# Token slots per work item in an expert loop: 128 becomes 96

## The chip, the core and the metric

The kernel runs on one core of a Trainium2 chip. The metric is the device time of one launch in microseconds (us). Of the kernel before there are three timed runs: 2023.76, 2024.81 and 2032.89 us, median 2024.81 us. The profile is one further execution, taken by the hardware profiler.

## What is computed

The reference is a chain of three transformer-like blocks on 256 tokens (plus 16 meta tokens in the first block) of width 1024, all in float32. The change touches one stage of the first block, the mixture of experts behind the pooling layer:

```python
def moe_swiglu(h, w_router, e_gate, e_up, e_down):
    logits = (h @ w_router).astype(jnp.float32)
    top_vals, top_idx = lax.top_k(logits, TOP_K)          # TOP_K = 2
    top_w = jax.nn.softmax(top_vals, axis=-1)
    combine = ...                                          # token x expert weights
    for e in range(N_EXPERTS):                             # N_EXPERTS = 8
        y = y + combine[..., e:e + 1] * swiglu(h, e_gate[e], e_up[e], e_down[e])
```

`swiglu` is `(silu(h @ w_gate) * (h @ w_up)) @ w_down` with a hidden width of 3584. Only the last 256 of the 272 tokens are needed from here on. Each of them goes to two experts, so there are 512 (token, expert) pairs for eight experts, 64 per expert on the average. The reference's router, evaluated on the inputs that the reference draws with seed 0, sends 47, 72, 65, 72, 61, 58, 74 and 63 tokens to the eight experts. With the seeds 1 to 5 the fullest expert gets 79, 92, 86, 76 and 93.

## The kernel before

**Precision.** Nearly all large products are split into three fast products. A float32 operand is taken apart into a high part, rounded to the fast float32 format (fp32r), and a low part, which is what the rounding lost. A product is then high x high + high x low + low x high, three matmuls that add into one PSUM bank.

**Weights.** A stream of chunks of 1 MB (128 partitions x 2048 float32) is fetched by the DMA queue of SyncE into a ring of six slots (`ring`). For each chunk ScalarE writes the high part (`split_moe`, L1592) into one of six other buffers (in the tiles `high` and `scr_r`), and VectorE writes the low part over the slot in the ring (`split_low`, L1935). TensorE then uses both. SyncE may refill a slot as soon as TensorE has begun on the chunk after it (semaphore `moe_begun`).

**Items.** The tokens are sorted by expert into 512 slots ahead of the loop (`sort_tokens`, L870). The loop works on items. An item is one expert and up to `CAP` of its slots. An expert with more than `CAP` tokens gets two items or more and its weights are fetched again for each; an expert with fewer still gets one. VectorE works out the number of items from the counts (`make_places`, `make_table`, L2047 to L2071), and every engine loops over that number, read from a register.

**Inside an item** there are 42 chunks in 14 units of 256 hidden columns (`UNITS`). In `gate_up` (L920, L923, L924) the stationary operand is the item's tokens, 128 input features x `CAP` tokens (`x_item_high`, `x_item_low`), and the moving operand is 512 columns of weights, so the result has `CAP` rows. ScalarE takes the silu of the gate half (L1611), VectorE multiplies by the up half (L2135). `turn_hidden` (L931) transposes the result by two TensorE transposes into PSUM, 128 hidden x `CAP` tokens each. ScalarE and VectorE take their high and low parts from there (L1598, L2123). In `down` (L945, L948, L949) these are the stationary operand, and the weights with 512 columns are the moving one. Once per item TensorE also makes the matrix that puts the rows back to their tokens (L962), and adds the previous item's outputs into `x` (`sum_outputs`, L894, L895, and L2106 on VectorE).

**Between items** ScalarE scales the finished rows (L1580) and VectorE takes their low part (L2112), and the next item's tokens are picked from the slots at a start read from a register (L1613, L2138, L2139). ScalarE also loads its function table for silu at the head of each item (L1584). Ahead of the first item the picks are made from PSUM (L1564 to L1569, L2084).

The order of the instructions on each engine is written out by hand. `MOE_ORDER` is the order of the chunks, and the splits run `LOOK` = 3 chunks ahead of TensorE. `ps[0:CAP, ...]`, `hid[0:CAP, ...]` and the like show that the rows of the hidden and of the output tiles are the item's slots.

Of the kernel before, what the change touches and what calls it, by code (L numbers as in the profile page):

```python
# [23 lines left out]
E_FF = 3584  # L24
KE = E_FF // P
NE = 8
CAP = 128
MAX_ITEMS = NE + 2 * SEQ // CAP
SLOTS = 2 * SEQ
WIDE = 256  # L30
# [169 lines left out]
def program(nc, w_stream, vec_in, h_in, out):  # L200
    with ExitStack() as ctx:
# [65 lines left out]
        x_tok_low = sq_old_r[:, 0:2 * D].rearrange("p (t d) -> p t d", t=2)  # L267
        slots_high = big[:, 0:KD * SLOTS + CAP]
        slots_low = big[:, 4224:4224 + KD * SLOTS + CAP]
        x_item_high = big_r[:, 8448:8448 + KD * CAP].rearrange("p (k c) -> p k c", k=KD)  # L270
        x_item_low = big_r[:, 9472:9472 + KD * CAP].rearrange("p (k c) -> p k c", k=KD)
        hn_old_r = hn_r[:, :, :].rearrange("p k t -> p (k t)")
        picks = hn_old_r[:, 1024:1024 + 2 * SLOTS + CAP]
        pick = picks[:, 0:2 * SLOTS].rearrange("p (t c) -> p t c", t=2)
# [2437 lines left out]
```

## Time and profile before

| | |
|---|---|
| median of three runs | 2024.81 us |
| span of the profiled execution | 2023.5 us |
| TensorE busy | 1981.8 us (98%), 12238 matmuls |
| VectorE busy | 1496.9 us (74%) |
| ScalarE busy | 1187.3 us (59%) |
| moved by DMA | 510.23 MB, mean 252 GB/s |
| experts' loop | about 378 to 1344 us of the span |

The spans are in microseconds from the first instruction. "PE" is the matmul side of TensorE and "PEld" its weight load, meaning the load of the stationary operand, which overlaps the matmul before it. A form such as `128*128 128x512` is the stationary operand (partitions * columns) and the moving one (partitions x columns). DVE is VectorE, ACT is ScalarE, POOL is GpSimd. A row of the windows view gives the stretch and its length, then the busy time of PE, PEld, DVE, ACT and POOL with the number of instructions, the granted clock as a share of full speed, the DMA share and GB/s; for one line alone only the engines that it runs on. The end of a matmul is modelled, its start is recorded, so the pace of TensorE is read from starts.

### The profile page before, as it was taken

The numbers are of one execution on the slowest core, as the hardware profiler recorded it, in microseconds if no ns is written. First come the engines' busy times: TensorE is split into PE (matmuls) and PEld (weight loads), VectorE is DVE, ScalarE is ACT, GpSimd is POOL, SyncE is SP. The second block draws the span as 40 slices with busy tenths as digits, with TensorE's granted clock in tenths as the row PEclk, the third lists the DMA queues.
The fourth block names the chain that finished last, engine by engine and source line by source line (L and its number), as shares of the span: only waits on it lengthen the run. The fifth ranks groups of instructions, "written<-read, shape, count | busy, mean of one in ns | idle before, by whom it ended". The sixth has DMA issues, their size and how long they took to land.

```text
span 2023.5 us, 31645 instructions
## 1 busy us (share of the span) xinstructions
PE 1981.8 (98%) x12238; PEld 1736.5 (86%) x12238; DVE 1496.9 (74%) x1628; ACT 1187.3 (59%) x1269; POOL 58.3 (3%) x105
## 2 busy tenths in 40 slices
PE   8999999999999999999999999999999999999997
PEld 7699998788888888888888888889978879989997
DVE  7776554888999999899899999977484358446652
ACT  5164443778777787777778777773363355325442
POOL 3020000000000000000000000010000000030000
PEclk9999999999999999999999999999999999999999
DMA  6535453499999999999999999974523324445551
GB/s 253 170 126 179 176 194 119 159 365 373 352 373 363 365 371 361 370 365 365 364 364 376 357 372 363 364 269 169 185 100 110 125 105 146 167 147 187 188 183 47
DMA packets 75863, 510.23 MB, mean 252 GB/s; under 512 B 8320, under 2 KB 14464, under 8 KB 14592
## 3 DMA queue, kind: packets, MB, share of 16 engines
q1 hardware_dynamic: 75776, 508.98, 67.7%
q8 instruction: 66, 1.08, 0.2%
q14 instruction: 21, 0.17, 0.0%
HBM read 506.66 MB, written 2.29 MB: 252 GB/s over the span
## 4 chain that ended last, share of the span: by engine, by line
PE 83%; DVE 5%; ACT 4%; issue 3%; DMA 3%; SPq 1%; POOL 0%; ACTq 0%; DVEq 0%; POOLq 0%
PE ps L920 9%; PE ps L924 9%; PE ps L923 9%; PE ps L652 8%; PE ps L655 8%; PE ps L656 8%; PE ps L945 4%; PE ps L949 4%; PE ps L948 4%; PE ps L629 3%; PE ps L1211 2%; PE ps L1214 2%; PE ps L1213 2%; DMA spread<-big 2%; PE ps L1146 1%
## 5 line engine op out<-in xcount | busy, mean ns | idle before, releaser
L1935 DVE TENSOR_TENSOR ring_r<-ring,high 128x2048 fp32r<-128x2048 f32 x227 | 517.8, 2290 | 53.6 <-ACT high L1592 32.7
L1592 ACT ACTIVATE high<-ring 128x2048 fp32r<-128x2048 f32 x224 | 428.6, 1913 | 15.1 <-DMA ring<-w_stream 14.7
L1808 DVE TENSOR_TENSOR ring_r<-ring,high 128x2048 fp32r<-128x2048 f32 x115 | 263.3, 2293 | 123.5 <-ACT high L1395 123.3
L923 PE MATMUL ps<-ring_r,big_r 128*128 128x512 f32 x896 | 349.1, 390 | 0.0
L655 PE MATMUL ps<-scr_r,high 128*128 128x256 f32 (+1 forms) x1200 | 342.6, 285 | 0.0
L1395 ACT ACTIVATE high<-ring 128x2048 fp32r<-128x2048 f32 x115 | 218.7, 1908 | 163.7 <-PE ps L652 92.3
L1935 DVE TENSOR_TENSOR ring_r<-ring,scr_r 128x2048 fp32r<-128x2048 f32 x112 | 256.4, 2290 | 39.0 <-ACT scr_r L1592 38.7
L652 PE MATMUL ps<-sq_r,high 128*128 128x272 f32 (+1 forms) x832 | 238.2, 286 | 5.5 <-DVE scr_r L1826 5.5
L656 PE MATMUL ps<-sq_r,ring_r 128*128 128x272 f32 (+1 forms) x832 | 237.7, 286 | 0.0
L655 PEld LDWEIGHTS ps<-scr_r,high 128*128 128x128 f32 x1200 | 227.1, 189 | 0.2
L1592 ACT ACTIVATE scr_r<-ring 128x2048 fp32r<-128x2048 f32 x112 | 214.5, 1915 | 17.8 <-DMA ring<-w_stream 17.8
L920 PE MATMUL ps<-high,big_r 128*128 128x512 f32 x512 | 205.2, 401 | 0.9 <-ACT big_r L1569 0.9
L924 PE MATMUL ps<-high,big_r 128*128 128x512 f32 x512 | 200.2, 391 | 0.0
L923 PEld LDWEIGHTS ps<-ring_r,big_r 128*128 128x128 f32 x896 | 168.8, 188 | 31.5
L652 PEld LDWEIGHTS ps<-sq_r,high 128*128 128x128 f32 x832 | 157.4, 189 | 6.7 <-issue 4.7
L656 PEld LDWEIGHTS ps<-sq_r,ring_r 128*128 128x128 f32 x832 | 157.0, 189 | 0.0
L920 PE MATMUL ps<-scr_r,big_r 128*128 128x512 f32 x384 | 154.1, 401 | 0.0
L924 PE MATMUL ps<-scr_r,big_r 128*128 128x512 f32 x384 | 150.1, 391 | 0.0
L924 PEld LDWEIGHTS ps<-high,big_r 128*128 128x128 f32 x512 | 96.1, 188 | 21.2
L920 PEld LDWEIGHTS ps<-high,big_r 128*128 128x128 f32 x512 | 96.2, 188 | 19.3 <-issue 1.4
L652 PE MATMUL ps<-hn_r,high 128*128 128x256 f32 (+1 forms) x368 | 109.3, 297 | 0.7 <-DVE scr_r L1832 0.5
L656 PE MATMUL ps<-hn_r,ring_r 128*128 128x256 f32 (+1 forms) x368 | 103.8, 282 | 0.0
(484 smaller groups left out, 3797.1 us busy)
## 6 DMA issues: line engine op xcount, KB each, us to landing
ring<-w_stream SPq DMA_DIRECT2D x477, 1024.0 KB, 4.8
big<-spread SPq DMA_DIRECT2D x32, 146.0 KB, 3.1
spread<-big SPq DMA_DIRECT2D x8, 151.0 KB, 5.4
h<-h_in SPq DMA_DIRECT2D x1, 1088.0 KB, 5.1
out<-hn SPq DMA_DIRECT2D x1, 1024.0 KB, 4.7
vec<-vec_in SPq DMA_DIRECT2D x1, 576.0 KB, 8.1
```

The costliest lines, as they stand in the source:

```text
L652: mm = pe.matmul(o, w_high[:, cols], x_high[:, k, 0:t], start=(k == 0), stop=False)
L655: pe.matmul(o, w_high[:, cols], x_low[:, k, 0:t], start=False, stop=False)
L656: mm = pe.matmul(o, w_low[:, cols], x_high[:, k, 0:t], start=False, stop=(k == kt - 1))
L920: mm = pe.matmul(o, x_item_high[:, k, :], w_high[:, cols], start=(k == 0), stop=False)
L923: pe.matmul(o, x_item_high[:, k, :], w_low[:, cols], start=False, stop=False)
L924: mm = pe.matmul(o, x_item_low[:, k, :], w_high[:, cols], start=False, stop=(k == KD - 1))
L945: mm = pe.matmul(o, hid_t_high[u % 3][:, kk, :], w_high[:, cols], start=first, stop=False)
L948: pe.matmul(o, hid_t_high[u % 3][:, kk, :], w_low[:, cols], start=False, stop=False)
L1395: act.activation(parts_at(c, 0, CH)[0], blocks_at(c, 0, CH), ACT.Copy).then_inc(S["weights_high"], 1)
L1592: act.activation(w_high, w, ACT.Copy).then_inc(S["moe_high"], 1)
L1808: dve.tensor_tensor(w_low, blocks_at(c, 0, CH), w_high.bitcast(F32), ALU.subtract).then_inc(S["weights_low"], 1)
L1935: dve.tensor_tensor(w_low, w, w_high.bitcast(F32), ALU.subtract).then_inc(S["moe_low"], 1)
```

## The change

One constant: `CAP`, the number of token slots of an item, goes from 128 to 96. Everything else follows from it.

```diff
@@ -24,7 +24,7 @@
 E_FF = 3584
 KE = E_FF // P
 NE = 8
-CAP = 128
+CAP = 96
 MAX_ITEMS = NE + 2 * SEQ // CAP
 SLOTS = 2 * SEQ
 WIDE = 256
```

What follows from it:

- The stationary operands of `gate_up`, `down` and L962 have 96 columns instead of 128. Their moving operands keep 512 (144 in L962) columns.
- `turn_hidden` transposes 96 rows instead of 128. The stationary operand is then 96 partitions * 128 columns, the moving one 96 x 96 (a corner of the identity) instead of 128 x 128.
- `sum_outputs` multiplies over 96 partitions instead of 128.
- ScalarE and VectorE handle 192 elements per partition instead of 256 in L1598 and L2123, and 768 instead of 1024 in L1613 and L2138. In L1611, L2135, L1580 and L2112 the elements per partition stay, on 96 partitions instead of 128.
- `make_places` compares the counts with 96 and also with 192 (the loop of L2048 now runs once; before it was empty): one more VectorE instruction on 128 x 8.
- `MAX_ITEMS` goes from 12 to 13. An expert with more than 96 tokens now takes a second item.

## Rows read from the trace of the kernel before

**Rows 1.** The page: busy time and granted clock in tenths, 40 slices.
```profile
PE 1981.8 (98%) x12238; PEld 1736.5 (86%) x12238; DVE 1496.9 (74%) x1628; ACT 1187.3 (59%) x1269; POOL 58.3 (3%) x105
...
PEclk9999999999999999999999999999999999999999
```

**Rows 2.** Windows: engines' busy time (instructions), clock, DMA share, GB/s; two items, ten us.
```profile
741.90:862.30 120.40, 120.32 (x551) 99.10 (x550) 109.49 (x82) 91.33 (x75) 0.00 (x0) 1.00 0.96 366
862.30:982.80 120.50, 120.40 (x551) 99.11 (x550) 109.62 (x82) 91.32 (x75) 0.00 (x0) 1.00 0.96 365
...
700.00:710.00 10.00, 10.00 (x46) 8.25 (x45) 9.64 (x9) 7.89 (x7) 0.00 (x0) 1.00 1.01 389
```

**Rows 3.** Chain of waits inside an item: start us, us, what.
```profile
691.07 0.23 PE ps L923
...
696.74 0.23 PE ps L924
696.97 0.22 PE ps L931 x2
```

**Rows 4.** Windows over the whole loop, for L920 alone and for L948 alone.
```profile
378.00:1345.00 967.00, 359.26 (x896) 168.34 (x896) 1.00 0.96 364
...
378.00:1345.00 967.00, 174.28 (x448) 84.14 (x448) 1.00 0.96 364
```

**Rows 5.** Groups by line and form, weight loads: count, busy us, mean ns.
```profile
L923 PEld LDWEIGHTS ps<-ring_r,big_r 128*128 128x128 f32 x896 | 168.8, 188 | 31.5
...
L722 PEld LDWEIGHTS ps<-big 128*32 128x32 f32 x384 | 13.0, 115 | 14.1 <-DMA big<-spread 4.9 <-issue 1.3
...
L1135 PEld LDWEIGHTS ps<-h,big 128*64 128x64 f32 x144 | 7.6, 136 | 2.3 <-issue 2.0
```

**Rows 6.** Chain of waits in stages with 128 x 256 moving operands.
```profile
1389.95 0.12 PE ps L652
...
1396.00 0.12 PE ps L652
...
1579.87 2.16 PE ps L629 x10
```

**Rows 7.** Timeline of weight loads around a pair of transposes: start us, us.
```profile
696.58 0.37 PEld L931 LDWEIGHTS ps<-ident,h 128*128 128x128 f32 x2
696.92 0.19 PEld L920 LDWEIGHTS ps<-high,big_r 128*128 128x128 f32 x1
697.03 0.19 PEld L923 LDWEIGHTS ps<-ring_r,big_r 128*128 128x128 f32 x1
```

**Rows 8.** Groups by line and form, matmul side of the small products.
```profile
L931 PE MATMUL ps<-ident,h 128*128 128x128 f32 x224 | 43.1, 274 | 2.4 <-DVE h L2135 2.1
...
L962 PE MATMUL ps<-h_r 128*128 128x144 f32 x16 | 3.4, 294 | 0.0
```

**Rows 9.** Timeline of TensorE at the first transposes of an item.
```profile
755.54 0.39 PE L924 MATMUL ps<-scr_r,big_r 128*128 128x512 f32 x1
756.01 0.44 PE L931 MATMUL ps<-ident,h 128*128 128x128 f32 x2
```

**Rows 10.** Chain of waits that leads to those transposes.
```profile
733.98 1.06 ACT big_r L1613
...
736.73 0.37 ACT h_r L1598
...
753.00 0.42 DVE big_r L2123
```

**Rows 11.** Groups of one item, 741.9 to 862.3 us, ScalarE and VectorE.
```profile
L1592 ACT ACTIVATE high<-ring 128x2048 fp32r<-128x2048 f32 x28 | 53.6, 1914 | 1.7 <-DMA ring<-w_stream 1.6
...
L1613 ACT ACTIVATE big_r<-big 128x1024 fp32r x1 | 1.1, 1055 | 0.0
...
L2106 DVE TENSOR_TENSOR x<-ps,x 128x512 f32<-128x512 f32 x4 | 2.7, 683 | 0.0
...
L2123 DVE TENSOR_TENSOR big_r<-ps,big_r 128x256 fp32r<-128x256 f32 x5 | 2.1, 418 | 0.0
```

**Rows 12.** Timeline of VectorE ahead of the loop.
```profile
382.39 2.29 DVE L1935 TENSOR_TENSOR ring_r<-ring,high 128x2048 fp32r<-128x2048 f32 x1 [1.48 <-ACT high L1592]
```

**Rows 13.** Chain of waits around a change between 128 and 46 stationary columns.
```profile
303.98 2.72 PE ps L792 x12
306.70 0.32 PE ps L652
```

## The prediction

> **What bounds the kernel now.** I read the page first. TensorE is busy for 98% of the span, at the upper of its two clock levels (2.4 GHz) nearly throughout [rows 1]. The windows of two whole items come next: an item takes 120.4 to 120.5 us, in which TensorE is busy for all but 0.1 us, VectorE for 109.5 us and ScalarE for 91.3 us, while the DMA engines are busy for 0.96 of the time and move 366 GB/s [rows 2]. So TensorE sets the pace and three other resources stand close behind it. The chain of waits says the same: inside an item it is an unbroken row of matmuls. The reader is to see the pace there: from the start at 691.07 to that at 696.74 lie 25 matmuls with 512 moving columns, 5.67 us, which is 227 ns each [rows 3]. The number of such matmuls in the loop is 3 x 896 (L920, L923, L924) + 3 x 448 (L945, L948, L949) = 4032 [rows 4], and 4032 x 0.227 = 915 us of the 966 us from 378 to 1344. The rest of an item is 28 transposes, 16 products of `sum_outputs`, two of L962, and one short wait.
>
> The number of items is 896 / 112 = 8, since an item has 14 x 8 = 112 matmuls of L920 [rows 4]. So no expert had more than 128 tokens.
>
> **The change part by part.**
>
> *Number of items.* The counts of the reference's router stand ahead of this text. The fullest expert has 74 of 96 slots with seed 0, and 93 with the worst of six seeds. I take 8 items again. A ninth would cost another 120.4 us [rows 2]; that is a rival below.
>
> *The 4032 large matmuls.* The moving operand stays at 512 columns, and what shrinks is the stationary one. Its load shrinks with it: 188 ns for 128 columns, 136 for 64, 115 for 32 [rows 5], so about 0.8 ns a column and an estimated 162 ns for 96. But the load of one matmul runs beside the matmul ahead of it, and back to back loads of 128 columns follow one another by 0.11 us [rows 7], half of the 227 ns that a matmul needs. The load is hidden before and after. If nothing else hangs on it, this part is worth 0.
>
> The part of the 227 ns that the moving columns don't explain decides here. 512 columns at 2.4 GHz are 213.3 ns, so 13.7 ns are left. In a stage with 256 moving columns of the same format, 51 matmuls take 6.05 us, 118.6 ns each against 106.7 ns of columns: 11.9 ns are left. In full float32 256 columns take 216 ns [rows 6], which is twice 106.7 with 2.7 ns left. So the fast format has a rest of 12 to 14 ns a matmul that hardly depends on the moving columns. It may belong to the change of stationary operand, and then it may shrink with its columns. The nearest rows all have 128 stationary columns, so I bound it: nothing at one end, and a quarter of 13.7 ns at the other, 3.4 ns x 4032 = 13.8 us. On the cost side no mechanism in these rows makes a narrower operand slower, save a change of mode (a rival below). I take 0, because the load has half of the period to spare; the other end goes into the range and is a rival.
>
> The trace has a load that costs 0.8 ns a column and is hidden. The Trainium skill ("TensorE: Matmul & The Clock Gate", on LDWEIGHTS and on the back-to-back gap) puts a load at its columns over 1.2 GHz and a gap at the moving columns over 2.4 GHz and some 2.5 ns, so it speaks against any gain here. By that rule 512 columns would take 216 ns; the trace agrees for full float32 and disagrees for the fast format, with 227 ns.
>
> *Transposes.* A pair is 2 of the 224 of L931 [rows 8]. The two of a pair start 0.11 us apart and so do the loads behind them [rows 3, 7]. Two things give that same 0.11 us: the moving side (128 columns of float32, by the pace of 216 ns for 256 [rows 6]), and the load of 128 columns [rows 7]. After the change the moving side has 96 columns (81 ns). The load of the second transpose still has 128 columns, since the hidden tile is the stationary operand, so the first one keeps its 108 ns. Behind the second comes a load of 96 columns (81 ns), so it falls from 108 to 81. That is 27 ns a pair, x 112 = 3.0 us. The ends are 0 (both bound by something that stays) and 6.0 us.
>
> *L962.* Two products an item with 144 moving columns (60 ns) behind loads of 128 columns (108 ns), which become 96: 2 x 27 ns x 8 = 0.4 us. `sum_outputs` keeps 128 columns on the stationary side and 256 on the moving side: 0.
>
> *ScalarE and VectorE.* Slopes from the rows of one item: ScalarE (1914 - 1055) / 1024 = 0.84 ns an element, VectorE from PSUM (683 - 418) / 256 = 1.04 ns [rows 11]. So L1613 saves 256 x 0.84 = 215 ns, each L1598 54 ns, each L2123 66 ns. Inside an item all of this is hidden by TensorE. It shows only where TensorE waits: at the first transposes of an item, which start 0.47 us behind the matmul ahead of them instead of 0.23 [rows 9], 0.24 us late. The chain that leads there goes through L1613, L1598 and L2123, once each [rows 10], 335 ns of saving against 240 ns of wait. TensorE itself comes some 0.1 us earlier by its own savings in the 22 us between, so the wait just closes. Over seven boundaries that is 7 x 0.24 = 1.7 us. What is late next is TensorE itself. The same chain stands ahead of the sums behind the last item: 0.3 us. Ahead of the first item two copies of 256 elements (L1566, L1569) become 192: 2 x 0.054 = 0.1 us.
>
> *The added VectorE instruction* (0.2 us with its wait) sits ahead of the loop, in a run of small ones behind which VectorE stands idle for 1.48 us until ScalarE's first split [rows 12]. That idle time hides it; without it, 0.2 us.
>
> *DMA and SyncE.* Not one transfer changes. SyncE waits for TensorE's begun chunks, so it issues earlier as TensorE gets faster. An item shorter by 0.6 us asks for 367 GB/s; ten us of the loop already ran at 389 [rows 2]. So this is no bound at this size of gain, and it would be none at 2 us more an item (373 GB/s).
>
> *Sum.* 3.0 + 0.4 + 1.7 + 0.3 + 0.1 = 5.5 us. The profiled span is 2023.5 us, the median of the runs 2024.8, so 1.3 us lie around the span. 2023.5 - 5.5 + 1.3 = 2019.3 us.
>
> **The rivals.**
>
> *B, the matmuls themselves get faster.* The rest of 12 to 14 ns shrinks with the stationary columns. For it: the rest doesn't follow the moving columns. Against it: full float32 has the same loads and a rest of 2.7 ns [rows 6]. Price at a full quarter: 13.8 us more, 2005.5 us; at half of that 2012.4.
>
> *C, slower: 96 is a mode of its own.* The trace shows that a switch between 128 and 46 stationary columns stops TensorE. Twelve products of L792, the last four with 46 columns, take 2.72 us instead of 12 x 0.216 = 2.59, and the matmul behind them takes 0.32 instead of 0.13 [rows 13]. That is 0.32 us for there and back. If 96 columns (or 96 partitions) were treated like 46, each pair of transposes and each `sum_outputs` would be an island among the 96-wide matmuls: 14 + 2 = 16 islands an item, 16 x 0.32 x 8 = 41 us, so 2019 + 41 = 2060 us. It decides as soon as the array is not used as a whole at 96. Against it: 96 is over half of the array, and two products of 96 can't stand side by side in it.
>
> The rows show a drain at a switch. The Trainium skill ("TensorEngine Tiling (Array Packing)", Key Properties) has the rule that changing the tiling mode drains TensorE, and among its modes there are sizes of 32, 64 and 128, but none of 96. By that, 96 stays in the whole-array mode and C costs nothing; no run here shows it yet.
>
> *D, slower: a ninth item.* One expert with more than 96 tokens: 120.4 us, so 2140 us. Only with other inputs than those counted.
>
> *E, nothing moves.* The transposes are held by something that stays, and the wait at the boundary moves to another engine: 2024.8 us.
>
> **How the numbers follow.** The forecast (case A) has 0.65, B 0.2, C 0.05, D 0.03, E 0.07. A measurement of this kernel tells about 0.5% (10 us) from no change, so the border is at 2014.7 us. B is faster by more than that (0.2), and I add 0.02 for the low end of A. A and E are within it: 0.7. C and D are slower: 0.08. The range goes from the full end of B, 2005, to 2027, which is E and the 2 us by which a median can lie above this one. C and D are left out.
>
> **What would show it.** The starts of the large matmuls still 227 ns apart (A) or down to 224 (B). The pairs of transposes: second one 27 ns shorter. The item at 119.8 us instead of 120.45. The first transposes of an item on time. Loads with 96 columns at about 162 ns. Eight items, so 896 matmuls of L920. A gap of over 300 ns behind each pair would be C. The prediction is wrong if the pace of the large matmuls changes in either direction, which is 0.5% for every 2.5 ns.

## The result

The change made the kernel slightly slower. The median of 15 runs is 2030.25 us against 2024.34 us for the kernel before; the ratio is 1.0026 with a 95% interval of 1.0019 to 1.0034. I had forecast 2019.3 us and a range up to 2027. The profiled execution took 2029.1 us from first to last instruction, against 2023.5.

Page of the kernel after, busy times, then windows of two items (PE, PEld, DVE, ACT, POOL, clock, DMA share, GB/s):

```profile
PE 1989.0 (98%) x12238; PEld 1630.2 (80%) x12238; DVE 1487.0 (73%) x1629; ACT 1179.2 (58%) x1269; POOL 58.2 (3%) x105
```
```profile
743.84:865.01 121.17, 121.17 (x551) 85.69 (x550) 108.24 (x81) 90.20 (x75) 0.00 (x0) 1.00 0.95 363
865.01:986.25 121.24, 121.24 (x551) 85.61 (x550) 108.27 (x81) 90.59 (x75) 0.00 (x0) 1.00 0.96 363
```

Every side but one does less in an item: the weight loads fell from 99.1 to 85.7 us an item, VectorE from 109.5 to 108.2, ScalarE from 91.3 to 90.3 [rows 2]. Only the large matmuls take longer. ("Large" is short for the 4032 matmuls of the loop with 512 moving columns.) An item takes 121.2 us instead of 120.4, with TensorE never idle, at the same clock, and there are still 8 items.

The chain of waits inside an item, and the weight loads around the pair of transposes in it:

```profile
646.13 0.23 PE ps L924
646.37 0.17 PE ps L931 x2
646.53 0.24 PE ps L920
646.77 0.23 PE ps L923
...
651.39 0.23 PE ps L945
```
```profile
645.97 0.37 PEld L931 LDWEIGHTS ps<-ident,h 96*128 96x128 f32 x2
646.29 0.16 PEld L920 LDWEIGHTS ps<-high,big_r 128*96 128x96 f32 x1
646.37 0.16 PEld L923 LDWEIGHTS ps<-ring_r,big_r 128*96 128x96 f32 x1
```

From 646.77 to 651.39 there are 20 large matmuls in 4.62 us: 231 ns each, where [rows 3] had 227. A pair of transposes has shrunk from 0.22 to 0.17 us. The load behind the pair is followed by the next after 0.08 us; it was 0.11 [rows 7].

Adding up the distances between the starts of all matmuls of the loop, by what stands at the two ends, gives the whole difference. The loop is from the first large matmul of `gate_up` to the last of `down`:

| from start to start | count | before, us | after, us | change |
|---|---|---|---|---|
| large matmul to large matmul | 3791 | 863.61 | 878.00 | +14.39 |
| the same, the first one right behind a transpose or L962 | 112 | 35.03 | 32.24 | -2.79 |
| first to second transpose | 112 | 12.71 | 9.83 | -2.88 |
| large matmul to first transpose (holds the waits) | 112 | 30.03 | 27.79 | -2.24 |
| products of L962 | 16 | 2.09 | 1.68 | -0.41 |
| all else | | 21.90 | 21.88 | -0.02 |
| the loop | | 965.37 | 971.42 | +6.05 |

In front of the loop 0.2 us were gained and behind it 0.3; between the runs of this document these two parts vary by up to 2 us, so both are within the noise. The 3791 distances have a mean of 227.8 ns before and 231.6 ns after. So the gains that I had counted are there, and more than those; 14.4 us of slower matmuls outweigh them.

### The profile page after: what moved, and what is told of

The parts are those of the page before. It is cut to its first block, busy times and chain, and to the rows that moved or that the text cites. A ratio compares the mean times of both kernels' runs of the same rounds, so it can differ in the third digit from the quotient of the medians.

```text
span 2029.1 us, 31646 instructions
## 1 busy us (share of the span) xinstructions
PE 1989.0 (98%) x12238; PEld 1630.2 (80%) x12238; DVE 1487.0 (73%) x1629; ACT 1179.2 (58%) x1269; POOL 58.2 (3%) x105
## 4 chain that ended last, share of the span: by engine, by line
PE 88%; DVE 5%; DMA 3%; issue 1%; ACT 1%; SPq 1%; POOL 0%; DVEq 0%; ACTq 0%; POOLq 0%
PE ps L924 10%; PE ps L920 10%; PE ps L923 10%; PE ps L652 8%; PE ps L655 8%; PE ps L656 8%; PE ps L945 5%; PE ps L949 5%; PE ps L948 5%; PE ps L629 3%; PE ps L1211 2%; DMA spread<-big 2%; PE ps L1214 2%; PE ps L1213 2%; PE ps L1146 1%
## 5 line engine op out<-in xcount | busy, mean ns | idle before, releaser
L923 PE MATMUL ps<-ring_r,big_r 128*96 128x512 f32 x896 | 351.9, 393 | 0.0
L920 PE MATMUL ps<-high,big_r 128*96 128x512 f32 x512 | 205.5, 401 | 0.8 <-ACT big_r L1569 0.8
L924 PE MATMUL ps<-high,big_r 128*96 128x512 f32 x512 | 202.4, 395 | 0.0
L923 PEld LDWEIGHTS ps<-ring_r,big_r 128*96 128x96 f32 x896 | 145.5, 162 | 55.0
L920 PE MATMUL ps<-scr_r,big_r 128*96 128x512 f32 x384 | 154.0, 401 | 0.0
L924 PE MATMUL ps<-scr_r,big_r 128*96 128x512 f32 x384 | 151.9, 396 | 0.0
L924 PEld LDWEIGHTS ps<-high,big_r 128*96 128x96 f32 x512 | 82.7, 162 | 36.2
L652 PE MATMUL ps<-hn_r,high 128*128 128x256 f32 (+1 forms) x368 | 109.5, 298 | 0.7 <-DVE scr_r L1832 0.5
L920 PEld LDWEIGHTS ps<-high,big_r 128*96 128x96 f32 x512 | 82.7, 162 | 31.9 <-issue 1.3
```

Of the source, the lines that this page charges most:

```text
L652: mm = pe.matmul(o, w_high[:, cols], x_high[:, k, 0:t], start=(k == 0), stop=False)
L920: mm = pe.matmul(o, x_item_high[:, k, :], w_high[:, cols], start=(k == 0), stop=False)
L923: pe.matmul(o, x_item_high[:, k, :], w_low[:, cols], start=False, stop=False)
L924: mm = pe.matmul(o, x_item_low[:, k, :], w_high[:, cols], start=False, stop=(k == KD - 1))
```

## The experiments

The question was why a matmul with 512 moving columns starts 4 ns later when its stationary operand is narrower. In the kernel after two things changed at once: the operands are 96 columns wide, and they start 96 columns apart instead of 128.

### Wide operands, 96-row transposes (wide_ops)

The edit, on the kernel after, cut down to one line of each sort. In this cut and those below, constants of the kernel are written out as their numbers:

```diff
-        x_item_high = big_r[:, 8448:8448 + KD * CAP].rearrange("p (k c) -> p k c", k=KD)
+        x_item_high = big_r[:, 8448:8448 + KD * 128].rearrange("p (k c) -> p k c", k=KD)
...
-                    o = ps[0:CAP, u % 2, :]
+                    o = ps[0:128, u % 2, :]
...
-                    act.activation(hid_t_high[u % 3].rearrange("p k c -> p (k c)"), ps[:, 2, 0:2 * CAP], ACT.Copy)\
+                    act.activation(hid_t_high[u % 3][:, :, 0:CAP], ps[:, 2, 0:2 * CAP].rearrange("p (k c) -> p k c", k=2), ACT.Copy)\
```

(The same for `x_item_low`, `hid_t_low` and the outputs of `down`. Inside the loop the last 32 columns are never written, and they hold old numbers.)

> Items hold 96 tokens and the transposes and copies work on 96 rows, as in the kernel after, but every stationary operand of the large products is again 128 columns wide and 128 apart (its last 32 columns hold old numbers, whose rows are never used). Theory W (the pace of the large matmuls depends on the width of the load): pace back from 231 to 227 ns, which gives back 13 to 16 us of the loop, while the pairs of transposes keep their 48 ns of saving (5.4 us) and the boundary waits stay closed: 2015 to 2018 us, below both kernels. Theory T (the narrower transposes or the shorter copies upset the pace of what follows them): pace stays near 231 ns, 2030 us.

Measured: 2020.79 us, ratio to the kernel before 0.9979 (0.9965 to 0.9993). The mean distance of the large matmuls is 227.8 ns again, so it is neither the narrow transposes nor the shorter copies that slow the matmuls. It is the fastest version here; the loop alone took 961.9 us, 3.5 less than before. But it came out 3 to 6 us above the 2015 to 2018 us that I expected. The trace shows two terms of this, together some 4.5 us. The pair of transposes with the matmul behind it took 427 ns instead of 403 in the kernel after (451 before), because the load behind the pair has 128 columns again. And the waits ahead of the first transposes came back, 3.7 us over the loop against 1.9 in the kernel after. TensorE's loads and matmuls around a pair:

```profile
643.82 0.37 PEld L932 LDWEIGHTS ps<-ident,h 96*128 96x128 f32 x2
644.13 0.19 PEld L921 LDWEIGHTS ps<-high,big_r 128*128 128x128 f32 x1
644.24 0.19 PEld L924 LDWEIGHTS ps<-ring_r,big_r 128*128 128x128 f32 x1
```
```profile
PEld ps L932 <- DVE h L2137: 2.2, 5, 0.5
```
```profile
PEld ps L931 <- DVE h L2135: 2.5, 5, 0.6
PEld ps L931 <- DVE h L2135: 0.5, 2, 0.3
```

The loads are 0.11 us apart, as in [rows 7]. The second fence is the waits view of weight loads over the later items: 2.2 us in 5 waits for the product of VectorE, the longest 0.5 us. The third has the same wait in the kernel before and in the kernel after.

### Narrow operands, old distance (stride128)

```diff
-        x_item_high = big_r[:, 8448:8448 + KD * CAP].rearrange("p (k c) -> p k c", k=KD)
+        x_item_high = big_r[:, 8448:8448 + KD * 128].rearrange("p (k c) -> p k c", k=KD)
...
-                        mm = pe.matmul(o, x_item_high[:, k, :], w_high[:, cols], start=(k == 0), stop=False)
+                        mm = pe.matmul(o, x_item_high[:, k, 0:CAP], w_high[:, cols], start=(k == 0), stop=False)
```

> The kernel after, with stationary operands of 96 columns, but their starts 128 columns apart (512 bytes) as before, in place of 96 (384 bytes). Theory A (the addresses make the pace): 227 ns, 2015 to 2018 us. Theory W (the width makes it): 231 ns, 2028 to 2032 us.

Measured: 2024.21 us, ratio 0.9998 (0.9979 to 1.0017). Both theories missed: the mean distance is 230.1 ns, between the two. The loop took 966.1 us. From wide_ops to this kernel only the width changes, and it costs 2.3 ns; from this one to the kernel after the start addresses change, and they cost 1.5 ns. This split holds for this order of the two steps alone: wide_at96, below, takes them the other way round and finds 4.2 ns for the addresses and -0.4 for the width.

### The disputed matmuls by themselves (m_quiet, m_noise)

These kernels compute nothing of the reference; each ran once. Each stretch is this loop, with its own width W and distance S (in columns of 4 bytes):

```python
for r in range(4):
    for k in range(8):
        at, wc = k * S, slice((k % 4) * 512, (k % 4 + 1) * 512)
        pe.matmul(o, x_high[:, at:at + W], w_high[:, wc], start=(k == 0), stop=False)
        pe.matmul(o, x_high[:, at:at + W], w_low[:, wc], start=False, stop=False)
        pe.matmul(o, x_low[:, at:at + W], w_high[:, wc], start=False, stop=(k == 7))
```

> A kernel that computes nothing of the reference: 14 stretches of 96 matmuls with 512 moving columns in the fast format, in the pattern of the expert loop, nothing else running. They differ in the width of the stationary operand (128, 120, 112, 96, 80, 64), the distance of its starts (128, 96, 160), and whether a pair of transposes stands in every 24 matmuls. Theory W: 227 ns at 128 wide whatever the distance, near 231 at 96 whatever the distance. Theory A: 227 at distance 128, 231 at distance 96. Theory N (the other engines and the DMA take turns with the loads): all near one value here, below 227 ns and the same for 96 and 128.

> The same 14 stretches, while ScalarE copies 128 x 2048 tiles, VectorE subtracts 128 x 2048 tiles and the DMA queue fetches chunks of 1 MB without pause. It also computes nothing of the reference. Theory N: the stretches get slower than in the quiet one and 96 wide differs from 128 only here. Theories W and A: the same differences between the stretches as in the quiet one.

Measured, view of one line each: duration in ns (least, median, most), first and last start in us. The first matmul of each of the 32 triples has its own line, so 93 matmuls lie between its first and last start. First the quiet one, four stretches, then three of the noisy one:

```profile
L273 PE MATMUL ps<-w_high,x_high x32: 389/389/389, 21.7 to 42.8; 128*128 128x512 f32 x32
L282 PE MATMUL ps<-w_high,x_high x32: 389/392/398, 43.4 to 65.0; 128*96 128x512 f32 x32
L291 PE MATMUL ps<-w_high,x_high x32: 390/392/398, 65.7 to 87.1; 128*96 128x512 f32 x32
L300 PE MATMUL ps<-w_high,x_high x32: 389/395/404, 87.8 to 109.3; 128*128 128x512 f32 x32
```
```profile
L273 PE MATMUL ps<-w_high,x_high x32: 389/389/389, 21.1 to 42.2; 128*128 128x512 f32 x32
L282 PE MATMUL ps<-w_high,x_high x32: 389/392/398, 42.8 to 64.4; 128*96 128x512 f32 x32
L291 PE MATMUL ps<-w_high,x_high x32: 390/392/398, 65.1 to 86.5; 128*96 128x512 f32 x32
```

L273 is 128 wide at distance 128: 21.1 us / 93 = 227 ns. L282 is 96 wide at 96, L291 96 wide at 128, L300 128 wide at 96. From the starts, whose own resolution is 1 ns, the means are 226.8, 231.8, 230.1 and 231.8 ns. The loop in the kernels has 231.6 for the second and 230.1 for the third, so the small kernel shows the pace of the narrow operands as the large one does. For 128 wide at 128 it gives 226.8 where the loop has 227.8. So theory W misses (128 wide is not at 227 ns at every distance), and so does theory A (96 wide at 128 is not at 227 ns). The noisy kernel has the same means within 0.2 ns in all 14 stretches. Its window of 21 us in the first stretch:

```profile
22.00:43.00 21.00, 21.00 (x94) 17.39 (x93) 21.00 (x10) 21.00 (x13) 0.00 (x0) 1.00 0.99 405
```

VectorE and ScalarE were busy throughout and the DMA moved 405 GB/s, more than the loop's 366, and the matmuls came no later. (The transfers ended at about 302 us, so the last of the 14 stretches, from 312 us, and a part of the one ahead of it ran without them.) Theory N falls. The other widths, all at distance 128, gave 233.3 ns for 120 columns, 228.9 for 112, 233.4 for 80 and 229.9 for 64. That is no straight line, and it isn't "narrower is slower". A pair of transposes in every 24 matmuls left the most frequent distances as they were (227 ns for 128 wide). But it slows some of the wide matmuls that follow: without the first one behind each pair, the mean for 128 wide at 128 was 228.4 ns with 128-row transposes and 227.6 with 96-row ones. These are the stretches to set beside the loop's 227.8. The narrow operands kept their means (231.7 and 230.1).

### Addresses (m_addr)

> A kernel that computes nothing of the reference: 21 stretches of matmuls with nothing else running. 15 have 512 moving columns in the fast format, with stationary operands 128 wide at one fixed address (0, 16, 32, 64 or 96 columns in), at distances 128, 192 and 256, with the moving operand 32 columns off, or 96, 104, 88 and 32 wide at distances 128, 256 and 0; three have 256 moving columns (128 and 96 wide); three are in full float32 with 256 moving columns. Theory P (the read of the stationary operand meets that of the moving one in a pattern set by its length and by how far its address moves from one load to the next): 227 ns for 128 wide at distances 128, 256 and 0, near 232 at 192; 96 wide near 230 at distances 256 and 0; 256 moving columns show the same differences of 2 to 5 ns, full float32 none (216 ns for all three). If only the alignment of the address counts, fixed addresses 16, 32 and 96 columns in are slower than 0, and 192 is like 96 apart.

Measured means for 512 moving columns, from the starts; "offset" is the start of the stationary operand in columns of 4 bytes, fixed for the stretch:

| stretch | ns |
|---|---|
| 128 wide, offset 0 / 64 | 226.7 / 226.8 |
| 128 wide, offset 16 / 32 / 96 | 233.4 / 232.4 / 232.4 |
| 128 wide, distance 128 / 192 / 256 | 226.7 / 227.0 / 226.7 |
| 128 wide, distance 128, moving operand 32 columns off | 232.3 |
| 96 wide, offset 0 / 32 | 230.0 / 231.6 |
| 96 wide, distance 256 | 230.0 |
| 104 / 88 / 32 wide, distance 128 | 229.0 / 233.3 / 231.5 |
| 256 moving columns: 128 at 128 / 96 at 96 / 96 at 128 | 119.8 / 117.8 / 116.0 |
| full float32, 256 moving columns, the same three | 215.8 / 215.8 / 215.8 |

The two stretches in full float32 with 128 and with 96 stationary columns take the same 20.5 us each:

```profile
L435 PE MATMUL ps<-raw x96: 378/379/379, 385.6 to 406.1; 128*128 128x256 f32 x96
L441 PE MATMUL ps<-raw x96: 379/379/379, 406.4 to 426.9; 128*96 128x256 f32 x96
```

How far the operand moves from load to load doesn't count, against theory P (192 is fast). Its place does: starts at multiples of 64 columns (256 bytes) gave 227 ns, those at 16, 32 and 96 gave 232 to 233. Starts 96 apart hit a multiple of 64 every other time, but that alone doesn't give their pace. The mean of an aligned and an unaligned start would be 229.6 ns for 128 wide and 230.8 for 96 wide, and both were measured at 231.8 (so was 128 wide at distance 160, in m_quiet). Nor are the distances in such a stretch of two sorts: at 128 wide and 96 apart, those in which an aligned start is loaded have a mean of 230.8 ns and the others 232.8, where stretches of one sort alone have 226.7 and 232.4. How such a mixture of starts comes to its number stays open. With 256 moving columns the size that I expected came (3.8 ns, within 2 to 5) and the sign did not: I had expected the same differences as at 512, and here the narrow operand is the faster one. Full float32 shows no difference, as expected.

### Is narrow slow as such? (m_beat)

> A kernel that computes nothing of the reference: 20 stretches of matmuls with nothing else running, to see whether narrow is slow as such. Theory P (a pattern of two reads that meet, set by lengths and addresses): which of 128 and 96 wide is faster changes with the number of moving columns (512: 128 wide by 3.3 ns; 256: 96 wide by 3.8 ns, both measured), so among 448, 384, 320 and 272 moving columns there are stretches of either sign; 124, 126 and 127 wide are slower than 128 by 2 ns or more each; and operands that are both 32 columns off are near 232 ns like one alone, or at 227 if only their distance from each other counts. Theory W2 (a narrower load is slower by itself, but for 256): 96 wide is slower by 2 to 4 ns at 448, 384 and 320.

Measured, 128 columns wide against 96, both at distance 128: 206.6 against 202.7 ns with 448 moving columns, 173.4 / 175.0 with 384, 146.7 / 146.6 with 320, 125.3 / 126.7 with 272. The rows for 448:

```profile
L337 PE MATMUL ps<-w_high,x_high x32: 362/368/369, 164.4 to 183.6; 128*128 128x448 f32 x32
L346 PE MATMUL ps<-w_high,x_high x32: 362/364/371, 184.2 to 203.0; 128*96 128x448 f32 x32
```

19.2 us against 18.8 us for the same work. So theory W2 falls: the sign changes with the number of moving columns. 127 columns wide took 226.7 ns, 126 took 233.3 and 124 took 228.3; my "2 ns or more each" held for one of three.

The stretch with both operands 32 columns off is the telling one. One alone off costs 5.6 ns; both off are at 226.7 ns:

```profile
L283 PE MATMUL ps<-w_high,x_high x32: 389/389/393, 42.9 to 64.0; 128*128 128x512 f32 x32
L292 PE MATMUL ps<-w_high,x_high x32: 391/394/399, 64.6 to 86.3; 128*128 128x512 f32 x32
```

L283 has both 32 columns off, L292 the stationary operand 32 and the moving one 64 off (233.3 ns). So for 128 wide and 512 moving columns, what counts is where the two operands stand to each other, by multiples of 64 columns. A 96 wide operand at distance 128 with the moving one 64 off had its 230.0 ns too. Only offsets that are multiples of 16 were tried.

### Back in the kernel: wide but 96 apart (wide_at96)

```diff
-                        mm = pe.matmul(o, x_item_high[:, k, :], w_high[:, cols], start=(k == 0), stop=False)
+                        mm = pe.matmul(o, big_r[:, 8448 + k * 96:8448 + k * 96 + 128], w_high[:, cols], start=(k == 0), stop=False)
```

(And in this manner for the other operands of `gate_up` and `down`; the 32 extra columns are the neighbour's, and their rows are not used.)

> Like wide_ops (items of 96, stationary operands 128 wide), but the operands start 96 columns apart as in the kernel after, so each load reads 32 columns of its neighbour. If the pace of the small kernels is that of the loop, the large matmuls start 231.8 ns apart, 4 ns x 4032 = 16 us more than in wide_ops: 2036 to 2038 us, the slowest of all. If the width alone counts, 227.8 ns and 2021 us.

Measured: 2034.53 us, ratio 1.0049 (1.0032 to 1.0066), mean distance 232.0 ns. The loop takes 975.5 us against 961.9 in wide_ops, 13.7 us for addresses alone, with the same widths: 16.0 us of slower matmuls, less 2.0 us of waits that closed (1.7 us instead of 3.7). It is the slowest version, as expected, 1.5 us below the range, which these waits account for. And beside the kernel after (231.6 ns, the same starts and 96 wide) it shows that with starts 96 apart the width makes no difference, as in the small kernels (231.8 and 231.8).

### Items of 112 (cap112s)

```diff
-CAP = 96
+CAP = 112
```

(With starts 128 columns apart.)

> Items of 112 slots, stationary operands 112 wide and 128 apart, for which the small kernel showed 228.9 ns. Theory P: pace 229 ns, 1.2 ns x 4032 = 4.8 us over the kernel before; a pair of transposes with the load behind it saves 24 to 26 ns x 112 = 2.8 us, and half of the waits at the item boundaries close (1 to 1.5 us): 2022 to 2027 us. If the pace fell in a straight line between 128 and 96 columns at this distance (226.8 to 230.1), 228.5 ns, which this run cannot tell apart; if width did not count at all, 226.8 ns and 2016 to 2019 us.

Measured: 2028.53 us, ratio 1.0022 (1.0013 to 1.0032), mean distance 229.5 ns. This is 1.5 us above the range that I gave. Its profiled execution is at the low end of its runs (2025.65 us), and its loop took 967.6 us, 2.2 more than before: +6.5 for the 3791 distances, -1.7 right behind the pairs and L962, -1.4 in them, -1.2 in the waits. The distances account for the trace; the rest of the median isn't explained by it.

## Why the prediction was wrong

**Number of items: right.** 8, as read from the router's counts.

**Loads of 96 columns: right.** An estimated 162 ns; measured, in the groups by line and form:

```profile
L920 PEld LDWEIGHTS ps<-high,big_r 128*96 128x96 f32 x512 | 82.7, 162 | 31.9 <-issue 1.3
...
L931 PEld LDWEIGHTS ps<-ident,h 96*128 96x128 f32 x224 | 31.0, 141 | 20.4 <-DVE h L2135 3.8
```

**The 4032 large matmuls: wrong, and this decided.** The step that failed is the one that bounded the rest of 12 to 14 ns: "On the cost side no mechanism in these rows makes a narrower operand slower" and then "I take 0, because the load has half of the period to spare". The load is hidden, that part was right, but the period isn't the sum of independent parts. What the load reads still moves the matmul that it hides behind: 226.7 ns with 128 columns, 230.0 with 96 at a good address, 231.8 with 96 at starts 96 apart (m_quiet, m_addr). For the place of the operand this is shown, since moving its start changes nothing but where the load reads. For the width it is argued: no run separates the narrower load from the narrower array and output behind it. I had no row with another width in this format, and my own rule was to bound such a price on both sides. I excluded a loss without a row that excludes it. A symmetric bound of +/- 3.4 ns, from the same 13.7 ns, would have given 2005 to 2033 us, with the result in it. Rows that hinted at it were in the trace: the rest was 13.7 ns at 512 moving columns, 11.9 at 256 and 2.7 in full float32 [rows 3, 6], so it wasn't a constant and wasn't only the load.

The Trainium skill ("TensorE: Matmul & The Clock Gate", on the back-to-back gap) has a gap of the moving columns over 2.4 GHz and some 2.5 ns for a single matmul. In the same place it says that in a stream of weight loads and matmuls the spacing is set by both; the prediction took up the first sentence and not the second. In full float32 the gap for a single matmul is what all stretches show at either width (215.8 ns for 256 columns in two cycles each). In the fast format none of the 34 plain stretches with 512 moving columns (m_quiet, m_addr, m_beat) comes near its 216 ns; they lie between 226.7 and 233.4.

**Transposes: right in kind, too small.** 27 ns a pair forecast, 48 measured (451 to 403 ns from the first transpose to the second large matmul behind the pair), 5.4 us instead of 3.0, within the ends that I gave. The term that was mis-sized is the first transpose of a pair. I held it at 108 ns for the load of the second one, 128 columns wide. But the distance is 86 ns (85 in wide_ops) with that load unchanged at 128 columns. It went the way of the moving side, for which I had 81 ns. The load of a transpose is shorter than another of its width, as the row above shows: 141 ns for 128 columns, where others take 188 [rows 5]. The view of the line L931 in the trace before already had it:

```profile
L931 PEld LDWEIGHTS ps<-ident,h x224: 137/139/143, 387.9 to 1338.3; 128*128 128x128 f32 x112
```

The other half of the saving, behind the pair, is the narrower load that follows, as predicted: it is gone in wide_ops.

**L962: right.** 0.4 us forecast, 0.41 measured.

**Item boundaries: right number, wrong reason.** The waits ahead of the transposes, over all items, fell from 4.0 to 1.9 us, by 2.0, of which 1.8 lie at the boundaries, where 1.7 was forecast. The copies were shortened as forecast: L1613 by 217 ns, L1598 by 54 and L2123 by 68. But wide_ops has the same short copies and kept 3.7 us. There the matmuls are at the old pace; in the kernel after and in wide_at96 they are slower by 4 ns, so TensorE comes some 0.35 us later to the wait (some 90 matmuls in the 22 us), and finds the operand ready. In stride128, slower by 2.3 ns, 2.2 us were left. So most of the closed wait is the other side of the slower pace. The forecast let TensorE come 0.1 us earlier by its own savings; wide_ops shows some 0.15 us of wait left at most boundaries, where some 0.24 were.

**Added VectorE instruction, DMA, SyncE: right.** The start of the loop moved by -0.2 us, less than it varies between runs, and the DMA followed with 363 to 368 GB/s.

**Rival C** (a mode of its own for 96) did not occur: the matmuls right behind a pair come earlier than before, not 0.3 us later. Rival B asked the right question about the rest of 13.7 ns and had the wrong sign for it.

## What to carry to other kernels

A weight load that is fully hidden can still set the pace of the matmuls over it. In the fast float32 format, with a stationary operand per matmul, 1 ns at 4032 matmuls is 4 us here. With 512 moving columns, keep both operands at starts that differ by multiples of 64 columns: that is worth 5.6 to 6.7 ns at 128 wide and 1.6 at 96. Measure a new width in a small kernel of a hundred matmuls before it is built in. Plain stretches gave the loop's pace within 0.2 ns for 96 wide and for starts 96 apart, 0.6 low for 112 wide and 1.0 low for 128 wide, so put the transposes of the loop into it as well. When a shape is made smaller, take the saving where it is direct (transposes, copies) and leave the wide operand as it is: that version is 0.2% faster than before, the full change 0.3% slower. And a term with no row of its own gets a bound on both sides, however plainly its cost seems to be hidden.

## What the runs showed of the hardware that was not expected

- With 512 moving columns in the fast format, the distance of two matmuls depends on the width of the stationary operand, and not in order: 128 wide 226.7 ns, 127 226.7, 126 233.3, 124 228.3, 120 233.3, 112 228.9, 104 229.0, 96 230.0, 88 233.3, 80 233.4, 64 229.9, 32 231.5.
- It depends on where the two operands stand to each other: at 128 wide 226.7 to 227.1 ns when their starts differ by a multiple of 64 columns, 232 to 233 when by 16 or 32 columns beyond that; at 96 wide 230.0 and 231.6. At 448 moving columns 96 wide is faster (202.7 against 206.6 ns), at 256 as well (116.0 against 119.8).
- Full float32 shows none of this: 215.8 ns for 256 moving columns in every case.
- Full loads of ScalarE, VectorE and, in the first twelve stretches and a part of the next, of the DMA beside it change none of the numbers of m_quiet (0.13 ns at most).
- What in the array or in its reads makes this pattern stays open. That the read of the stationary operand meets that of the moving one fits it in kind, since lengths and relative addresses count and the other engines and the DMA didn't. But no run here shows the reads themselves, and nothing here works out from it which width is fast, or the 231.8 ns of starts 96 apart.
